# Output projection of a Mamba-2 layer: one block that prepares the conditioning rows and the output weights itself, with the first tile multiplied piece by piece

## The reference, cut to what matters

```
mod = cs @ w_ada[i] + b_ada[i]
sh1, sc1, g1, sh2, sc2, g2 = jnp.split(mod, 6, axis=-1)
hm = x * (1.0 + sc1[:, None]) + sh1[:, None]
...
y = gated_group_rmsnorm(y.reshape(b, Lp, SSM_D_INNER), z, norm_w)
return (y.astype(h.dtype) @ w_out)[:, :L]
...
x = layer_norm(DEEPNORM_ALPHA * x + (1.0 + g1[:, None]) * y, ln_g[i, 0], ln_b[i, 0])
hm = x * (1.0 + sc2[:, None]) + sh2[:, None]
y = grouped_moe(hm, w_router, b_router, w_gate[i], w_up[i], w_down[i])
x = layer_norm(DEEPNORM_ALPHA * x + (1.0 + g2[:, None]) * y, ln_g[i, 1], ln_b[i, 1])
```

## Time and profile before

| | |
|---|---|
| median of 3 runs | 3112.36 us (3112.1 to 3117.61) |
| the profiled execution: its time | 3118.38 us |
| its span, first to last instruction | 3116.6 us |
| busy share of the span | PE 89%, DVE 71%, POOL 49%, ACT 42% |
| mean granted TensorE clock | 0.942 of full |

### The profile page before, as it was taken

The page is one execution under the profiler, slowest core; times in us unless marked ns, Lnnn a source line. Parts: engine busy times, 40 slices in busy tenths (PEclk is TensorE's granted clock), DMA queues, the critical chain, the costliest instruction groups (busy, mean ns, idle before and its releaser), DMA issues. The chain is left out here.

```text
span 3116.6 us, 41489 instructions
## 1 busy us (share of the span) xinstructions
PE 2785.0 (89%) x14798; PEld 2330.0 (75%) x14798; DVE 2224.6 (71%) x2623; ACT 1298.8 (42%) x1624; POOL 1514.7 (49%) x817
## 2 busy tenths in 40 slices
PE   7599999999999999999938999967999999999910
PEld 2288888888888888888816888856888888888810
DVE  2567778777787778787742333456888888888868
ACT  1233333333333333333331111115777767776722
POOL 0023343333433343433401222216899999999965
PEclk9799999999999999999958999978999999999955
DMA  6754544445444544445142323228887878678667
GB/s 233 301 199 163 206 169 160 163 172 203 170 165 164 205 169 160 163 172 190 54 155 90 115 102 107 95 95 297 329 319 267 296 264 322 238 267 292 244 232 242
DMA packets 249588, 619.01 MB, mean 199 GB/s; under 512 B 15346, under 2 KB 97906, under 8 KB 240756
## 3 DMA queue, kind: packets, MB, share of 16 engines
q1 hardware_dynamic: 225556, 530.27, 47.4%
q0 software_dynamic: 11520, 41.95, 4.0%
q10 hardware_dynamic: 12384, 45.09, 3.6%
HBM read 609.65 MB, written 99.88 MB: 228 GB/s over the span
## 5 line engine op out<-in xcount | busy, mean ns | idle before, releaser
L1515 DVE TENSOR_TENSOR piece_lo<-piece_raw,piece_hi 128x2048 fp32r<-128x2048 f32 x187 | 563.2, 3031 | 102.4 <-ACT piece_hi L1620 102.3
L1620 ACT CAST piece_hi<-piece_raw 128x2048 fp32r<-128x2048 f32 x280 | 526.2, 1909 | 205.7 <-DVE ye L1680 156.0
L1515 POOL TENSOR_TENSOR piece_lo<-piece_raw,piece_hi 128x2048 fp32r<-128x2048 f32 x93 | 566.0, 6086 | 26.1 <-ACT piece_hi L1620 24.0
L572 PE MATMUL pj<-hm,w_hi 128*128 128x512 f32 x2048 | 533.4, 406 | 25.3 <-DMA hm<-hm_parts 22.0
L841 DVE SCALAR_TENSOR_TENSOR cv<-ub,par,cv 128x512 f32<-128x512 f32 x384 | 385.4, 1004 | 170.9 <-ACT cv L719 161.8
L572 PEld LDWEIGHTS pj<-hm,w_hi 128*128 128x128 f32 x2048 | 379.1, 190 | 101.3 <-DMA hm<-hm_parts 23.6
L536 POOL TENSOR_TENSOR xw<-xw,t 128x512 f32<-128x512 f32 x64 | 96.8, 1512 | 474.6 <-DVE t L907 474.6
L587 PE MATMUL pz<-wz_hi,hm 128*128 128x256 f32 x2048 | 294.7, 289 | 0.7
L587 PEld LDWEIGHTS pz<-wz_hi,hm 128*128 128x128 f32 x2048 | 264.4, 191 | 6.5 <-DVE wz_lo L819 3.5
L572 PE MATMUL pj<-hm,w_lo 128*128 128x512 f32 x1024 | 254.8, 391 | 0.0
L572 PEld LDWEIGHTS pj<-hm,w_lo 128*128 128x128 f32 x1024 | 192.2, 188 | 43.1
(11 more groups left out here) (292 smaller groups left out, 5881.7 us busy)
## 6 DMA issues: line engine op xcount, KB each, us to landing
hm<-hm_parts SPq DMA_DIRECT2D x32, 4096.0 KB, 13.3
piece_raw<-in_w_gate SPq DMA_DIRECT2D x94, 1024.0 KB
piece_raw<-in_w_up SPq DMA_DIRECT2D x94, 1024.0 KB
piece_raw<-in_w_down SPq DMA_DIRECT2D x92, 1024.0 KB
decay<-acum_rows SPq DMA_DIRECT2D x32, 1024.0 KB, 4.7
w_raw<-in_w_in SPq DMA_DIRECT2D x48, 512.0 KB, 7.6
expert_out<-ye ACTq DMA_DIRECT2D x46, 512.0 KB, 6.6
hm_parts<-hl SPq DMA_DIRECT2D x4, 4096.0 KB, 16.0
```

What stands on the lines that cost most here:

```text
L572: mm = nc.tensor.matmul(pj[m % 2][:], wp[m][:, kk, :], hm[b][:, hp, kk, :], start=q == 0, stop=q == 3 * KK - 1)
L1515: v.tensor_tensor(lo[q][:], raw[q][:], hi[q][:].bitcast(F32), ALU.subtract).then_inc(lo_done[q], 1)
L1620: nc.scalar.copy(hi[q][:], raw[q][:]).then_inc(hi_done[q], 1)
```

## The change

`row_vectors` is gone. `out_projection` takes over its work in one block:

- SP's order is now: first half of `y` tile 0, six pieces of `w_out`, second half of `y` tile 0, ten more pieces (each when its buffer is free), five broadcast rows, the router's weights and bias, and then the loop.
- The four rows are finished in columns: ACT's queue loads the biases as columns (16 KB), DVE adds them (three small instructions), PE turns the 128 x 32 columns by one transpose, ACT copies the result and stores it to DRAM (`adad`, 16 KB), and SP loads three of the rows broadcast from there. The fourth is loaded by `experts`. The 32 diagonal blocks, the 8 products and the 8 additions are not there any more, nor are the 8 bias rows.
- PE's first tile goes through `first_products`: for each piece `m` of `w_out`, as soon as its low part is done, the six products that use it.
- Four of the six `wraw` buffers share the memory of `yhi`/`ylo` of odd tiles, the other two are `r` and `h2`. So tile 1 is split, and `r` loaded, only when all 16 low parts of `w_out` are done.
- The mixing of rows (`mix_rows`) stands on DVE after the low halves of tile 1 and before the first tile's LayerNorm.
- In `experts` the masks have memory of their own; pieces 4 and 5 of the first expert tile are loaded, split and lowered ahead of the loop; DVE lowers pieces 0 and 1 before it waits for `ids`; SP waits for the first gather to land (`x_in[0]`) instead of for `ids_ready`.

```
 def first_products():
     for m in range(YTILES):
         pe.wait_ge(lo_done, 2 if m >= HALF else 1)
         pe.wait_ge(wo_lo_done, m + 1)
         for q, (yp, wp) in enumerate(((yhi, w_hi), (yhi, w_lo), (ylo, w_hi))):
             for n in range(2):
                 mm = nc.tensor.matmul(op[0][n][:], yp[0][:, m, :], wp[:, m, n * 512:(n + 1) * 512], ...
...
+            pe.wait_ge(cols_ready, 3)
+            nc.tensor.transpose(cand[0:4 * KK, 0:P], k.ada[:], k.ident[:]).then_inc(rows_tr, 1)
...
+            act.dma_start(adab[:], k.d["b_ada_cols"][:, 2 * KK:]).then_inc(bias_in, 16)
+            act.wait_ge(rows_tr, 1)
+            nc.scalar.copy(turned, cand[0:4 * KK, 0:P]).then_inc(rows_set, 1)
+            act.wait_ge(rows_set, 1)
+            act.dma_start(k.adad.rearrange("r (q t) -> (r q) t", t=P), turned).then_inc(rows_out, 16)
+            split_half(0, 0, 0)
+            for m in range(AHEAD):
+                high_w(m)
...
-            load(0, range(GU))
-            sp.dma_start(g2[:], k.g2d[0].partition_broadcast(P)).then_inc(g2_in, 16)
-            sp.wait_ge(ids_ready, 1)
+            load(0, range(PIECES))
+            sp.dma_start(g2[:], k.adad[3].partition_broadcast(P)).then_inc(g2_in, 16)
+            sp.wait_ge(x_in[0], 16)
             loop(sp, step)
...
             fetch(1, 1)
             low_part(pool, nc.gpsimd, 3, 0)
+            low_part(pool, nc.gpsimd, 5, 0)
```

More of the change, by code:

```diff
@@ L984, in _ @@
                     gate_by_sigmoid(i, 3)
[L987 to L1082, removed]
@@ L1106, in out_projection @@
         flat = yraw[:].rearrange("p m t -> p (m t)")
+        wraw = [w[:] for w in wraw + [r, h2]]
+        turned, adab = h2t[0:4 * KK, 0, :], rb
+        mixed = h2t[:].rearrange("p q t -> p (q t)")
+        wo_in = [sem(f"wo_in{b}") for b in range(AHEAD)]
+        (bias_in, wo_hi_done, wo_lo_done, cols_ready, rows_tr, rows_out, rows_set, row_in, mix) = (sem(n) for n in (
+            "bias_in wo_hi_done wo_lo_done cols_ready rows_tr rows_out rows_set row_in mix").split())
         eq = flat[:, 0:NE]
@@ L1149, in step @@
                     load_y(i + 1, 0)
+                if not in_loop(i, 1):
+                    sp.wait_ge(wo_lo_done, YTILES)
                 if in_loop(i, 1):
@@ L1185, in products, with first_products @@
                 mm.then_inc(o_mm, 1)
+            def first_products():
+                for m in range(YTILES):
+                    pe.wait_ge(lo_done, 2 if m >= HALF else 1)
+                    pe.wait_ge(wo_lo_done, m + 1)
+                    for q, (yp, wp) in enumerate(((yhi, w_hi), (yhi, w_lo), (ylo, w_hi))):
+                        for n in range(2):
+                            mm = nc.tensor.matmul(op[0][n][:], yp[0][:, m, :], wp[:, m, n * 512:(n + 1) * 512],
+                                                  start=m == 0 and q == 0, stop=m == YTILES - 1 and q == 2)
+                            if m == YTILES - 1 and q == 2:
+                                mm.then_inc(o_mm, 1)
             def turn(j):
@@ L1410, in choose @@
                     link(v.tensor_tensor(g, g, s, ALU.mult))
-            low(0, 0)
+            dve.wait_ge(bias_in, 16)
+            for cols, one in ((slice(0, KK), 1.0), (slice(KK, 2 * KK), 0.0), (slice(2 * KK, 4 * KK), 1.0)):
+                nc.vector.scalar_tensor_tensor(out=k.ada[:, cols], in0=k.ada[:, cols], scalar=one,
+                                               in1=adab[:, cols], op0=ALU.add, op1=ALU.add
+                                               ).then_inc(cols_ready, 1)
+            low_half(0, 0, 0)
+            for m in range(AHEAD):
+                low_w(m)
+            low_half(0, 0, 1)
+            for m in range(AHEAD, YTILES):
+                low_w(m)
             loop(dve, step, 1)
```

111 lines of the change are left out of this document (80 added, 31 removed).

## The result

| | before | changed |
|---|---|---|
| median of 4 runs | 3112.84 us (3112.1 to 3117.61) | 3070.71 us (3069.26 to 3071.55) |
| profiled execution, span | 3116.6 us | 3069.7 us |
| mean granted TensorE clock | 0.942 | 0.951 |

The ratio is 0.9854, 95% interval 0.9842 to 0.9865; the medians are 42.1 us apart.

What follows compares the result with a forecast made beforehand. The uncovered 68.5 us from the weights' stage to the output projection's first product were to shrink to the transfers' pace: 42.5 - 0.9 - 0.9 + 3.3 = 44.0 us gained, giving a 3068.4 us median, range 3061 to 3080.

Steps and rivals of the forecast that it cites:

- The pace of the transfers: New block: SP's transfers set its length; 24.25 units of 1.43 us, tile 1's first half of `y` landing at 1619.9.
- ACT's head: Block's start: columns' load 3.5 us and small steps 2.0 precede ACT's first split of `y`, at 1588.1.
- the late head: Rival: columns' load queues behind SP's transfers, first split at 1596, stream loses 5 to 7 us; time 3074; 12 in 100.
- PE's first tile and the clock: Output projection: tile 0's 96 products take 22 us at full clock, end at 1613.7, and are not the bound.
- The rival of the low clock: PE stays at the lower clock through the first tile, which ends at 1635.3; time 3073.7; 1 in 10.
- the clause that `h2` would wait: In the low-clock rival: `h2` waits for tile 1's products, whose second half starts at 1649.2, 5.3 us later.
- Tile 1, mixing, what is late next: Output projection: tile 1's second half starts at 1643.9, gain 42.5 us; PE waits 1.4 for `h2`, 0.9 for tile 2.
- Clearing: Stage ends: 15 more semaphores cleared ahead of the experts, at 0.06 us each, cost 0.9 us.
- The experts' start: First gather lands sooner because SP's loads wait for it: gain 3.3 us, between 0 and 3.3.
- three times nothing: Experts' start: DVE's two low parts moved ahead, SP's later gate pieces and POOL's earlier piece 5 each change nothing.
- The whole: Whole kernel: gain of 44.0 us, from the median to 3068.4 us.

Runs made afterwards that it cites:

- `y` before rows: Changed kernel, but SP loads the first half of `y` of tile 1 ahead of the five rows: 3070.14 us, ratio 0.9846.
- all four edits: Changed kernel with piece 5's split back in the loop, SP on the ids, tile 1's first `y` half before the rows, mixing between tile 1's halves: 3059.68 us.
- low parts back: Changed kernel, but DVE's low parts of pieces 0 and 1 again behind the ids; SP still waits for the gather: 3075.29 us, ratio 0.9866.
- SP on `ids`: Changed kernel, but SP waits for the ids again instead of the gather's landing: 3074.25 us, ratio 0.9864.
- piece 5 in the loop: Changed kernel, but POOL's split of piece 5 of the first expert tile is back in the loop's first step: 3070.3 us, ratio 0.9853.
- second measurement: The changed kernel run once more, unedited, beside the kernel before: 3070.31 us, ratio 0.9853.

## Why the prediction was right, and where it was not

*The pace of the transfers.* Right. Tile 1's first half was split at 1619.08, 37.4 us after the block's start; forecast was 1619.9 - 1582.6 = 37.3. From 1588 to 1613 the stream ran at 377 to 418 GB/s instead of 367, but it began later than assumed (41 GB/s from 1582 to 1583, 196 in the next us), and when the router's bias landed, at 1617.6, nothing was left of the lead. What the forecast did not have is that SP's issue of that bias, 16 KB, stood for 5.50 us, so that tile 1's half was issued at 1613.7 and not at 1608.7. It cost little here: the DMA engines were busy all the same (0.99 from 1613 to 1618), and the half landed 1.4 us after the bias, as the forecast has it for one unit. In other profiles it landed up to 2.4 us after it, so up to 1 us can hang on this. That the place in the stream counts, `y` before rows showed.

*ACT's head.* The columns' load took 5.3 us to land instead of 3.5, and the split of `y` began 6.8 us after the block's start instead of 5.5. This is a little of the late head; it cost nothing, since the stream did not run dry.

*PE's first tile and the clock.* It ended 34.5 us after the start (1616.23), forecast 31.1, and was not the bound: it began 1.3 us later and did its first pieces at the low level. The rival of the low clock did not happen: the granted clock read 0.65 from 1593 to 1598 and 1.00 after, and two products took 1.05 us first and 0.62 then. The Trainium skill, "TensorE: Matmul & The Clock Gate", section "HAM oscillation — how this bites in real kernels", speaks of a loop whose work is shorter than its wait for the next transfer. Here the first pieces ran at the low level, six products in 2.7 us where a piece lands each 1.3, and so left PE behind the transfers, with no waits. In the working of this rival the time is right, but not the clause that `h2` would wait: by its own numbers PE's products of tile 1, not `h2`, come last.

*Tile 1, mixing, what is late next.* Right in each term: the second half 60.6 us after the start instead of 61.3, waits of 1.34 and 0.90 instead of 1.4 and 0.9. The gain there is 103.9 - 60.6 = 43.3, forecast 42.5. Tile 2's wait is 0.8 to 1.1 us in every profile in which the mixing stands behind both halves and the first tile goes piece by piece; it is gone with the mixing between the halves and with all four edits.

*Clearing.* The experts' stage started 460.6 and 461.2 us after the block instead of 503.0 and 501.1: 41.1 on average, forecast 42.5 - 0.9 - 0.9 = 40.7. The clearing can be read from SP's wait at the stage's end before the experts (L89), from 2000 to 2120 us before and now:

```profile
SPq L89 <- PEq L89: 2.0, 1, 2.0
...
SPq L89 <- PEq L89: 3.0, 1, 3.0
```

1.0 us more, where 0.9 was forecast.

*The experts' start* is the step that failed, though its size came out by luck: forecast 3.3, measured 3.5 (895.4 and 891.9, the means of two profiles each). The prediction's words "SP's loads ... ran beside it. Now SP waits for it" name one edit where three act. Of the 7.7 us by which the gather comes sooner, 4.1 are DVE's low parts moved ahead of `ids` (low parts back), to which the prediction gave "nothing": it asked only what covers them, not what they had held up. The other 3.6 (37.4 against 33.8) are SP's loads, but only when the gather is late: with the low parts out of the way, SP may go on at `ids` and nothing changes (29.7). No run has the low parts back and SP on `ids` with all else as changed; that the 3.6 are the loads rests on the landing, 6.8 us after the end of the gather's instruction before and 3.2 with the low parts back, and on the second gather of SP on `ids`. And about 4 of the 7.7 were given back by two terms that were also priced at "nothing". POOL's low part of piece 5 makes DVE's low part of piece 2 4.5 us longer, SP issues the up pieces after it, and the second expert tile waits: 2.8 us of it came back at the last product when it was moved (piece 5 in the loop). And SP's wait for the gather, undone alone, gave 2.0 back (SP on `ids`); undone together, the two give 3.0. So +4.1, +3.6 and about -4 stand where the prediction had +3.3 and three times nothing.

*The whole.* Forecast 3068.4, measured 3070.71: 44.0 against 42.1 by the medians, 44.6 by those of the second measurement (3114.95 and 3070.31). The profiles give 41.1 + 3.5 = 44.6, and 45.4 from the block's start to the last instruction; the 0.8 between them falls behind the last product, where I looked for no cause. The difference lies inside what the mixer's end spreads.

## What to carry to other kernels

Where stages meet at barriers, ask for each side of the barrier which transfers and which small preparations wait there for no reason, and then sum the transfers in their issue order: that sum, not the products, gave the new block its length. An instruction that costs nothing where it stands may hold up another engine that works beside it, so for each one moved ask also what ran beside it before and what will now. When a median spreads more than an edit is worth, read both kernels' timelines from the start of the stage that the edit touches.

## What the runs showed of the hardware

The instruction that starts a gather on POOL was held by a DVE low part (a subtraction of two operands in SBUF, 2.28 us alone) that was running when it started. Each profile has 48 such gathers. The first one took 1.22, 3.12 and 5.24 us with none, one and two low parts beside it, and ended 1.1 us after DVE's last. Of the later ones, 624 started within a low part: they took 2.2 to 2.8 us and all ended 0.85 to 0.87 us after that low part's end, nearly all in the midst of the next. The 34 that started outside one took 0.96 to 0.99 us, and of these 12 had a low part begin beside them, in the closest cases 0.1 us after their start. So which of the two starts first decides. Why the stage's first gather waited for both low parts, and the later ones for one, no run shows. The Trainium skill, "SBUF — State Buffer", section "Who interferes with whom", says that a two-input instruction of DVE contends with reads of GpSimd. The 6.78 us against 2.28 of DVE's low part beside POOL's agree. The same section of the Trainium skill also reports from its own probe that `tensor_tensor` did not hold up transfers issued by GpSimd, and infers that descriptor generation needs another interface. The gathers here were held. They also read their row numbers from `ix`, and whether a plain transfer issued by POOL is held, no run here shows.

SP's issue of one 16 KB load, the router's bias, stood for 5.50 us with seven transfers of its queue not yet landed. In the twelve profiles with this order it stood for 4.8 to 6.3 us, with seven or eight of them; in the two of the kernel before, with one, for 0.57. Most issues in this block took 0.3 to 0.65 us, but there were also some of 1.1 and 1.2, and at the experts' start of 2.1 to 3.0. What exactly an issue waits for no run shows.

The end of the unchanged mixer lay within 11.2 us in 14 profiles (1576.1 to 1587.3). What sets it I did not look for. The granted clock adds its own spread: in three of eight profiles of the same output projection it fell once more within tile 2, and that tile's first half took 13.3 to 13.5 us instead of 11.8.
